# Top-k rounds of a two-block transformer kernel: where in VectorE's order the second and third tile's rounds stand

## What is computed

```python
def compress(kv, pe, w1, w2):
    ...
    return jax.nn.gelu(flat @ w1) @ w2
...
        logits = jnp.einsum('bqhd,bsd->bqhs', qib, k_idx).astype(jnp.float32)
        score = jnp.einsum('bqh,bqhs->bqs', wb.astype(jnp.float32) * idx_scale, jax.nn.relu(logits))
        score = jnp.where(key_pos[None, None, :] <= tq[None, :, None], score, -jnp.inf)
        _, sel = lax.top_k(score, k_top)
```

## Time and profile before

| what | value |
|---|---|
| median of 3 runs | 2203.53 us (2201.86 to 2203.97) |
| profiled execution | 2201.14 us, span 2199.1 us |
| mean granted TensorE clock of the span | 0.946 |
| attention stage in the span | 194 to 407 us |
| busy in the span | TensorE 92%, VectorE 43%, ScalarE 32%, GpSimd 8% |

### The profile page before, as it was taken

How to read it: one execution, slowest core, us unless ns; L and a number is a source line. 1 busy time by engine, 2 the same in 40 slices (tenths; PEclk the granted TensorE clock), 3 DMA queues, 4 the chain that set the end, 5 groups by cost and what they waited for, 6 DMA issues and landing times. The chain is left out here.

```text
span 2199.1 us, 25080 instructions
## 1 busy us (share of the span) xinstructions
PE 2031.7 (92%) x10202; PEld 1568.7 (71%) x10202; DVE 947.2 (43%) x1558; ACT 704.3 (32%) x1139; POOL 171.0 (8%) x142
## 2 busy tenths in 40 slices
PE   6998878989999998999999889995888899999999
PEld 3756645758888885888888666663777767888887
DVE  4454587364434335332333423346443454332332
ACT  3321356342323234221222435563111143221221
POOL 0003122200000010000001004340000010000000
PEclk8997589999999999999999999996998999999999
DMA  8543000112222221232232121100000022232231
GB/s 344 189 154 120 30 30 1 49 48 96 96 96 96 96 96 50 101 118 68 100 111 85 67 68 49 38 20 0 1 1 1 1 77 78 98 111 77 99 118 52
DMA packets 41585, 172.13 MB, mean 78 GB/s; under 512 B 4608, under 2 KB 4864, under 8 KB 38144
## 3 DMA queue, kind: packets, MB, share of 16 engines
q1 hardware_dynamic: 41472, 170.54, 22.2%
HBM read 168.43 MB, written 2.10 MB: 78 GB/s over the span
## 5 line engine op out<-in xcount | busy, mean ns | idle before, releaser
L319 PE MATMUL bank<-hs,wsp 128*128 128x512 f32 x1392 | 554.9, 399 | 20.0 <-DVE hs L1290 11.5
L320 PE MATMUL bank<-hs,wsp 128*128 128x512 f32 x1392 | 547.0, 393 | 0.0
L321 PE MATMUL bank<-hs,wsp 128*128 128x512 f32 x1392 | 546.6, 393 | 0.0
L893 ACT ACTIVATE wsp<-ring 128x1024 fp32r<-128x1024 f32 (+2 forms) x244 | 269.2, 1106 | 853.2 <-PE bank L321 850.9
L1251 DVE TENSOR_TENSOR wsp<-ring,wsp 128x1024 fp32r<-128x1024 f32 (+2 forms) x244 | 312.1, 1282 | 385.5 <-ACT wsp L893 384.9
L319 PEld LDWEIGHTS bank<-hs,wsp 128*128 128x128 f32 x1392 | 264.4, 190 | 99.5 <-issue 38.1
L320 PEld LDWEIGHTS bank<-hs,wsp 128*128 128x128 f32 x1392 | 264.7, 190 | 55.9 <-issue 1.9
L321 PEld LDWEIGHTS bank<-hs,wsp 128*128 128x128 f32 x1392 | 264.5, 190 | 56.1
L321 PE MATMUL bank<-hids,wsp 128*128 128x512 f32 x608 | 241.0, 396 | 0.0
L320 PE MATMUL bank<-hids,wsp 128*128 128x512 f32 x608 | 241.0, 396 | 0.0
L319 PE MATMUL bank<-hids,wsp 128*128 128x512 f32 x608 | 241.0, 396 | 0.0
(11 more groups left out here) (279 smaller groups left out, 2209.7 us busy)
## 6 DMA issues: line engine op xcount, KB each, us to landing
ring<-m_gate SPq DMA_DIRECT2D x44, 512.0 KB, 3.2
ring<-m_up SPq DMA_DIRECT2D x44, 512.0 KB, 3.2
ring<-m_down SPq DMA_DIRECT2D x32, 704.0 KB, 4.0
ring<-m_w_in SPq DMA_DIRECT2D x38, 512.0 KB, 3.3
arena<-ada_late SPq DMA_DIRECT2D x16, 1024.0 KB, 4.8
ring<-m_w_up SPq DMA_DIRECT2D x32, 512.0 KB, 3.2
ring<-m_w_down SPq DMA_DIRECT2D x32, 512.0 KB, 3.2
ring<-m_w_out SPq DMA_DIRECT2D x16, 512.0 KB, 3.4
```

Source lines behind the costliest of these rows:

```text
L319: pe.matmul(out, lhs[0], rhs[0], start=start, stop=False)
L320: pe.matmul(out, lhs[0], rhs[1], start=False, stop=False)
L321: return pe.matmul(out, lhs[1], rhs[0], start=False, stop=stop)
L893: act.activation(wsp[:, s % SPLIT, 0, 0:size], ring[:, i % RING, 0:size], ACT.Copy)\
```

## The change

```diff
--- before.py
+++ after.py
@@ -1501,7 +1501,8 @@
                 if p == 16:
                     lo(PINDEX["w_out", 2])
 
-                if rounds < 3 * ROUNDS and p >= 4 + rounds - ROUNDS:
+                due = ROUNDS if p < 2 else ROUNDS + 8 if p < 4 else 2 * ROUNDS + p - 4
+                while rounds < min(due, 3 * ROUNDS):
                     top_round(rounds)
                     rounds += 1
             outputs(NT - 1, 1)
```

## The result

| kernel | median | range | ratio to before |
|---|---|---|---|
| before, same chip | 2203.07 us | 2201.86 to 2203.97, 4 runs | |
| changed | 2186.72 us | 2185.23 to 2188.77, 4 runs | 0.9927 [0.9910, 0.9944] |

The change makes the kernel 16.4 us faster by the medians. The prediction was 8.5 us, to 2195.0, with 2190.5 as its lower end: the sign was right, and the size too small by about half. The profiled execution took 2188.77 us (span 2187.0) where that of before took 2201.14 (2199.1), 12.4 us less.

A forecast was written before the change was run, and what follows sets the result against it. In the attention stage VectorE was taken to set the pace from about pair 8 to 35, TensorE from 36. 2.8 lost - 10.3 freed = -7.5, with 1.0 of clock -8.5: 2203.5 to 2195.0 us, range 2190.5 to 2201.0.

The forecast's parts named there:

- The batches: Attention stage, behind pairs 2 and 4: eight rounds each cost 0 beside the compressions, 2.1 and 7.5 us left.
- rival C: Third tile: ScalarE or GpSimd replaces VectorE, or first batch overruns by 3 to 5 us; 2201.0 us, chance 0.20.
- The widened rounds: Pairs 5 to 20: rounds 512 wide in place of 384 lose 2.8 us up to pair 21.
- The freed rounds: Pairs 21 to 35 lose their round: -10.3 us, with TensorE becoming the bound in pairs 27 to 33.
- The clock: TensorE's low-clock stretches after the waits at 304.59 and 351.16 shorten: 0 to 3.6 us, 1.0 taken.
- predicted at one clock: Attention stage without any clock change: 2.8 us lost, 10.3 gained, sum -7.5 us.
- upper bound: Clock gain at most 3.6 us: 1.7 compressed scores, 1.3 two steps behind them, 0.6 scores at 308.82.
- Rival B: Attention stage: the clock pays in full, -7.5 - 3.6, to 2192.4 us, down to 2190.5; chance 0.17.
- The reference of the sum: Whole kernel: sum made against the profiled 2201.14 us, then applied to the median 2203.53, 2.4 above.
- D: Third tile: TensorE enters at low clock and stays, nine pairs +10.8, total +8.2, to 2211.7 us; chance 0.05.
- E: Attention stage: nothing comes through, as output steps and copies keep their pace; 2203.5 us, chance 0.03.

The follow-up runs named there:

- e4_all16_p2: Changed kernel with all sixteen rounds of tile 2 behind pair 2 and none in pass 4: 2188.45 us, 0.9939 of before.
- e5_two_each: Changed kernel without batches, the same 32 rounds placed two in each of passes 4 to 19: 2207.47 us, 1.0022 of before.
- e9_filler: Kernel before plus idle TensorE matmuls, three before the compressed scores of pairs 24 and 36, two before the last transposes: 2196.63 us, 0.9976.
- e12_after_filler: Changed kernel plus idle TensorE matmuls, one before the last compressed scores (pair 36), two before the last transposes: 2186.65 us, 0.9929 of before.
- e2_before: Kernel before, unedited, run as a kernel of its own and profiled again: 2202.07 us, 1.0000 of before.
- e3_batches: Changed kernel with only tile 2's batches kept, tile 3's rounds back in passes 20 to 35: 2192.96 us, 0.9959 of before.
- e8_spread: Changed kernel with eleven rounds behind each compression, the last ten in passes 6, 7, 23, 27 to 31 and two in 35: 2179.36 us, 0.9894.
- e6_fill: Changed kernel with eleven rounds in place of eight behind pairs 2 and 4, the other ten in passes 5 to 14: 2187.13 us, 0.9926.
- e10_spread_filler: e8_spread plus idle TensorE matmuls, one at pairs 24 and 36 each, two before the last transposes: 2181.37 us, 0.9906 of before.

## Why the prediction was right in sign and too small

**The batches: right.** Predicted 200.9 to 211 with 2.1 us left, and 215.9 to 226 with 7.5 left; measured 2.27 and 7.40. One sentence of this step was too narrow: each batch was given its own compression as cover, with up to 10 us at stake. e4_all16_p2 overran the first by 8 us and by the medians paid nothing, so the price of an overrun there, in rival C too, was a cost that isn't there. e5_two_each shows that the cover as a whole is what the change lives on.

**The widened rounds: right.** Predicted 2.8 us by pair 21; the mask of pair 21 begins at 298.39 for 295.15, 3.2 later, of which 0.3 is the later start of the stage. The compressed scores of the second tile were at the high clock in both profiles.

**The freed rounds: right.** From pair 28 on VectorE waits for TensorE's scores (0.42 and 1.84 us at the first two masks) and no longer the other way round, the period is 2.49 us for a predicted 2.55, and the last compressed scores wait 1.27 us for a predicted 1.1.

**The clock: the step that failed.** It was put as "at most 3.6 us, at least nothing. I take 1.0". Piece by piece, the measured shift of a row less the shift that was predicted at one clock:

| row of TensorE | before | after | shift | predicted at one clock | difference in this piece |
|---|---|---|---|---|---|
| third tile's compressed scores | 304.59 | 305.46 | +0.9 | -0.2 | +1.1 |
| transposes of pair 27 | 327.17 | 322.61 | -4.6 | -3.0 | -2.6 |
| transposes of pair 33 | 345.49 | 337.52 | -8.0 | -5.8 | -0.6 |
| last compressed scores | 351.16 | 341.54 | -9.6 | -7.5 | 0.0 |
| first w_out | 406.63 | 394.14 | -12.5 | -7.5 | -2.9 |

In sum -5.0 us, for the 1.0 that was taken. 0.6 of it is the period, where TensorE is at 1.00 in both kernels, so it is no clock; 0.4 of the +1.1 was there at mask 21. The rest, some 4.8 us, is put down to the clock, and its places can be read off the rows; it is a difference to a sum whose waits are themselves a prediction. The other 0.7 of the +1.1 are a cost of the clock: just ahead of the third tile the changed kernel runs at the low clock (301.43 to 304.7). In the third tile steps close to those of the earlier trace rows went from the low clock to the high one. The timeline of TensorE before:

```profile
306.73 1.11 PE L497 MATMUL bank<-cst,arena 128*128 128x128 f32 x4
307.77 1.12 PE L512 MATMUL bank<-tmp,arena 128*64 128x128 f32 x8
...
317.02 0.90 PE L497 MATMUL bank<-cst,arena 128*128 128x128 f32 x3 [2.19 <-DVE arena L1491]
317.85 1.12 PE L512 MATMUL bank<-tmp,arena 128*64 128x128 f32 x8
318.90 1.60 PE L481 MATMUL bank<-arena 64*128 64x384 f32 x4
```

From 317.02 to the next transposes (320.44) this took 3.42 us and takes 1.91 after (314.76 to 316.67), behind a wait of 0.68 us in place of 2.19. In the changed kernel TensorE doesn't wait from there to the last compressed scores, so these 1.5 us come through in full. In the fourth tile it is the scores of pair 39 and the steps ahead of them, while those of pair 40 took 1.13 us in both: TensorE's timeline of the kernel before, and then of the changed one, reads

```profile
364.47 0.94 PE L497 MATMUL bank<-cst,arena 128*128 128x128 f32 x4 [0.83 <-DVE arena L1491]
...
366.82 1.75 PE L481 MATMUL bank<-arena 64*128 64x512 f32 x4
...
370.55 1.13 PE L481 MATMUL bank<-arena 64*128 64x512 f32 x4
```

```profile
354.91 0.66 PE L497 MATMUL bank<-cst,arena 128*128 128x128 f32 x4 [0.83 <-DVE arena L1491]
...
356.30 1.13 PE L481 MATMUL bank<-arena 64*128 64x512 f32 x4
359.41 1.13 PE L481 MATMUL bank<-arena 64*128 64x512 f32 x4
```

3.73 us between these two for 3.11, and ahead of them 2.35 us from the transposes at 364.47 to 366.82 for 1.39 (354.91 to 356.30), both behind a wait of 0.83. And in the tail, after:

```profile
387.36 1.42 PE L497 MATMUL bank<-cst,arena 128*128 128x128 f32 x8 [1.98 <-ACT tmp L997]
388.71 1.09 PE L512 MATMUL bank<-tmp,arena 128*64 128x128 f32 x16
```

1.42 and 1.09 for 1.88 and 1.97, behind a wait of the same length (1.98 for 1.99); from there to w_out 6.78 us for 8.13. Of the places from which the prediction built its upper bound, the scores at 308.82 gave their 0.6 (0.92 for 1.52), the others nothing in sum: the compressed scores after 351.16 (3.18 now, for 3.88) and the two steps behind them (1.54 and 1.55, unchanged); the 0.7 that they gave, the scores behind them took back (1.88 at 347.60 for 1.13 at 357.92). So the bound was too low by its method: it priced only the low stretches next to the two longest waits, while low stretches stand behind middling waits too, and a shift of everything redraws all of them. Rival B was the nearest account, with 3.6 of clock; it would have given 11.1 us in all and come nearer to the measured 14 to 16 than the 8.5 taken, and even it stopped short. The rule beside it is that idle gaps between bursts of matmuls throw the array back to half clock (the Trainium skill, TensorE: Matmul & The Clock Gate, HAM oscillation). The runs agree with its direction, as e9_filler and the window at 1.00 show; behind two waits of the same length, though (1.99 and 1.98), the tail took 8.13 us in one kernel and 6.78 in the other, and no run shows what decides between the two.

That the clock is a cause and not only a companion is shown for the stretch behind mask 36: idle matmuls take 4.1 us off it in the kernel before and 1.5 in the changed one, and the 2.6 us between them are near the 2.9 of the table's last piece. For the third tile no run separates it; there it rests on the rows alone, which stand the same in two profiles of each kernel. The 4.3 us from the medians look like the 4.8 from the rows, but idle matmuls gained nothing ahead of mask 36, where 1.9 of the 4.8 lie, and the intervals are wide, so this agreement is in part luck. The two leave 7.7 and 9.7 us for the waits, where 7.5 were predicted; the 2 us between them stay open, and the clock's phase at pair 12 (1.3 us between the profiles of e9_filler and e12_after_filler by mask 13) is enough to blur them.

**The reference of the sum: the second miss.** The prediction took the profiled execution's distance to the median, 2.4 us, over unchanged. That execution had pair 12's compressed scores at the high clock; e2_before didn't, and was 2.6 us longer in the stage. The profiled execution of the changed kernel stands the other way round, 2.1 above its median. So 12.4 us between two profiled executions are 14.1 and 16.4 between medians, with intervals that overlap. Of the 7.9 us by which the forecast (8.5) fell short of the 16.4, some 3.9 are the profiled difference and the other 4 are this. What makes some executions of the changed kernel up to 3.5 us shorter than its profiled one no kept trace shows.

**The other rivals.** C didn't come: neither ScalarE nor GpSimd takes VectorE's place in pairs 27 to 33, TensorE does, as forecast. D's start came, TensorE at the low clock from 301.43 to 304.7, but it ended there (the compressed scores took 2.10), and the window from 305 is at 1.00. E is out by e3_batches and the result.

## What to carry to other kernels

Ask of each stage which engine waits, and put serial work of an engine under the longest stretch in which it waits for another; here the same 32 rounds made the stage 18.8 us longer in passes without that cover, and e8_spread, which uses every such place, is within 1.2 us of not doing the last sixteen at all (2179.4 us; it beats both kernels). A change that shortens TensorE's waits may also be paid in clock, here at steps behind middling waits (0.83 and 2.19 us) and not only beside the longest: count every step that stands at its low-clock duration, not the two that stand out, as far as TensorE is what bounds the stretch. Where VectorE did, at pair 24 of e9_filler, the high clock bought nothing. And profile the kernel before twice, before a sum is built on one execution.

## What the runs showed of the hardware

- One program, two profiles: 2.10 or 3.72 us for the same sixteen passes at one place, with 2.6 us in the stage's length, while the low-clock steps of the third and fourth tile were the same. In e6_fill (3.73), e9_filler and e10_spread_filler (3.72) the same place was at the low clock as well. Which phase is drawn wasn't tied to anything in the program.
- Idle matmuls that nobody reads made a kernel 5.4 us faster (0.9976 [0.9967, 0.9985]). In kernels with shorter waits the medians moved by 1.1 us for the better and 1.6 for the worse, within their intervals, while from the last compressed scores to w_out the traces took 1.5 and some 1.4 us less.
- TensorE is not only slow behind waits: in 198 to 212 it is busy for 14.00 of 14 us, with 128x64 matmuls, at granted clock 0.50, in both kernels.
